# A fused two-layer decoder step on one core: routing scores moved into the gate steps, rows fetched four dots ahead, loads in parts

## What is computed

```python
q = (xb @ w_q).reshape(PEER_BLOCK, PEER_HEADS, 2, PEER_HALF)
s1 = jnp.einsum('thd,kd->thk', q[:, :, 0], sub_k1).astype(jnp.float32)
s2 = jnp.einsum('thd,kd->thk', q[:, :, 1], sub_k2).astype(jnp.float32)
v1, i1 = lax.top_k(s1, PEER_TOPK)
v2, i2 = lax.top_k(s2, PEER_TOPK)
cand = (v1[..., :, None] + v2[..., None, :]).reshape(PEER_BLOCK, PEER_HEADS, PEER_TOPK * PEER_TOPK)
top_s, top_pos = lax.top_k(cand, PEER_TOPK)
eidx = jnp.take_along_axis(cand_idx, top_pos, axis=-1)
gate = jax.nn.softmax(top_s, axis=-1)
u = expert_u[eidx]
act = jax.nn.gelu(jnp.einsum('thkd,td->thk', u, xb))
vv = expert_v[eidx]
return jnp.einsum('thk,thkd->td', (gate * act).astype(vv.dtype), vv)
```

## Time and profile before

| what | value |
|---|---|
| median of 3 runs | 3708.06 us (3708.01 to 3715.67) |
| span of the profiled execution | 3715.8 us |
| time around the span in that execution | not listed apart; the slowest of the runs, 3715.67 us, is as long as this span |
| TensorE busy | 3517.8 us (95%) |
| VectorE, ScalarE, GpSimd busy | 2481.2, 1361.9, 1842.5 us |
| mean granted clock of TensorE | 0.975 of full speed |
| phases s0 with routing, about | 436 to 1173 us |
| phase y0, about | 1175 to 1757 us |
| the same in layer 1, about | 2368 to 3095 and 3097 to 3700 us |

### The profile page before, as it was taken

One profiled execution on the slowest core, in us unless ns is written; L12 is line 12 of the kernel. 1 busy time (PEld: TensorE's weight loads), 2 busy tenths in 40 slices (PEclk: granted clock), 3 DMA queues, 4 the chain that ended last, 5 costly groups with the idle time before them and its releaser, 6 DMA issues.

```text
span 3715.8 us, 61775 instructions
## 1 busy us (share of the span) xinstructions
PE 3517.8 (95%) x21277; PEld 3348.0 (90%) x21277; DVE 2481.2 (67%) x5400; ACT 1361.9 (37%) x1938; POOL 1842.5 (50%) x1172
## 2 busy tenths in 40 slices
PE   7999999999999999999888689999999999999998
PEld 7999999999999999999773359999999999999998
DVE  3342597777775777775678543679697876777774
ACT  3322343534444333333221353344435353333332
POOL 3434456555655555552541234456565655555551
PEclk9999999999999999999998699999999999999999
DMA  3222367877788999994346322467777879999982
GB/s 131 80 69 91 103 188 247 277 247 262 262 281 274 298 310 313 324 320 154 99 116 179 105 74 91 136 193 249 268 240 277 274 282 277 297 326 311 329 295 97
DMA packets 392484, 812.36 MB, mean 219 GB/s; under 512 B 52104, under 2 KB 249672, under 8 KB 384888
## 3 DMA queue, kind: packets, MB, share of 16 engines
q1 hardware_dynamic: 171600, 458.35, 37.0%
q0 software_dynamic: 64608, 230.73, 18.1%
q10 hardware_dynamic: 156048, 120.37, 11.0%
HBM read 695.39 MB, written 112.74 MB: 217 GB/s over the span
## 4 chain that ended last, share of the span: by engine, by line
PE 66%; DVE 16%; DMA 7%; issue 4%; ACT 2%; POOL 2%; SPq 2%; another core or an unknown queue 0%; ACTq 0%; DVEq 0%; POOLq 0%
PE acc L638 42%; PE acc L625 15%; DMA rows<-u_in,expertP 4%; PE misc L774 3%; DVE rows L1838 3%; DMA raw<-slabs_in 2%; POOL w_lo L2274 1%; DVE misc L1773 1%; DVE route L1777 1%; DVE hot_gate L1876 1%; PE misc L814 1%; ACT w_hi L1104 1%; DVE work L1716 1%; DVE keyi L1724 1%; PE misc L843 1%
## 5 line engine op out<-in xcount | busy, mean ns | idle before, releaser
L2274 POOL TENSOR_TENSOR w_lo<-raw,w_hi 128x1024 fp32r<-128x1024 f32 x365 | 892.6, 2446 | 1079.8 <-ACT w_hi L1104 1078.6
L638 PE MATMUL acc<-h_hi,w_hi 128*128 128x416 f32 x3072 | 1097.7, 357 | 0.2 <-POOL h_lo L2316 0.2
L638 PE MATMUL acc<-h_lo,w_hi 128*128 128x416 f32 x3072 | 1085.9, 353 | 0.0
L638 PE MATMUL acc<-h_hi,w_lo 128*128 128x416 f32 x3072 | 1081.2, 352 | 0.0
L1104 ACT ACTIVATE w_hi<-raw 128x1024 fp32r<-128x1024 f32 x617 | 653.3, 1060 | 1090.0 <-DMA raw<-slabs_in 1045.4
L638 PEld LDWEIGHTS acc<-h_hi,w_hi 128*128 128x128 f32 x3072 | 581.2, 189 | 8.5 <-POOL h_lo L2316 0.6
L638 PEld LDWEIGHTS acc<-h_hi,w_lo 128*128 128x128 f32 x3072 | 581.9, 189 | 7.4
L638 PEld LDWEIGHTS acc<-h_lo,w_hi 128*128 128x128 f32 x3072 | 581.3, 189 | 3.9
L1955 DVE TENSOR_TENSOR w_lo<-raw,w_hi 128x1024 fp32r<-128x1024 f32 x252 | 325.4, 1291 | 206.1 <-ACT w_hi L1104 205.5
L1838 DVE CUSTOM_DVE_ANT_0 rows<-acc,rows 128x1024 f32<-128x1024 f32 (+1 forms) x224 | 273.4, 1221 | 205.9 <-DMA rows<-u_in,expertP 183.7
L638 PE MATMUL acc<-y_hi,w_hi 128*128 128x416 f32 x1024 | 362.1, 354 | 10.3 <-DVE y_lo L1947 4.3
(11 more groups left out here) (349 smaller groups left out, 5549.4 us busy)
## 6 DMA issues: line engine op xcount, KB each, us to landing
raw<-slabs_in SPq DMA_DIRECT2D x617, 512.0 KB
act_d<-gelu SPq DMA_DIRECT2D x256, 208.0 KB
gate_d<-gout SPq DMA_DIRECT2D x52, 1024.0 KB
abuf<-act_d ACTq DMA_DIRECT2D x32, 1664.0 KB
gbuf<-gate_d ACTq DMA_DIRECT2D x30, 1664.0 KB
unit<-ck_in SPq DMA_DIRECT2D x72, 128.0 KB
vquad<-cv_in SPq DMA_DIRECT2D x64, 128.0 KB
unit<-ck_in ACTq DMA_DIRECT2D x56, 128.0 KB
```

The source lines that it names most:

```text
L638: last = pe.matmul(acc[:, 0, par, 0:ND], w[:, c, :], m(c), start=c == 0 and w is w_hi[r] and m is m_hi, stop=c == KC - 1 and w is w_lo[r])
L2274: pool.tensor_tensor(w_lo[r][:], raw[r][:], w_hi[r][:].bitcast(F32), ALU.subtract).then_inc(lo_done, 1)
```

## The change

The edits are in the PEER part alone, and the same for both layers:

- Scores. Block 0's scores stay at the start. Those of block 1 go out in two pairs after slabs 18 and 20, those of blocks 2 and 3 in quarters of four products behind gate steps 4, 7, 10 and 13 of the block before, all through one bank (`quarter_scores`). ACT takes each quarter (`take_scores`), and may overwrite `sc` once `sums_done` says that VectorE has the candidates of the block before.
- Gate steps in three blocks of 16, at slabs 40, 72 and 104; the last 4 of the 52 at slabs 120 to 123 (`LAST_STEPS`). The four steps of block 0's tokens are the first of block 1's sixteen.
- Dots. 16 in the first window (twelve between the parts of `routing`, four behind it), 8 in each later one, 24 in each block of gate steps. In block 1's window the dots begin at the eighth place, and `expertP` is made at the fifth.
- Fetches. The fetch of row i goes out where dot i - 4 stands in the table, the first four at step 5; rows of groups 1 and up not before step 28.
- `hot_gate` is made from `iota` in SBUF and no longer from its copy in `misc`.
- Values: twelve in eleven slabs; groups begin and end at steps that a table gives.
- `act_d` and `gate_d` have other layouts: gates are stored in pieces of 512 bytes (8 KB before) and read in pieces of 3 KB and more (512 bytes before).
- A group's loads in y0 are eight parts spread over seven slabs. The last part of the first group's gates is loaded at step 124 (121 before), and group 1's parts at steps 124 to 126.
- The gelu of the dots and the product `weights` come after the first group's `weigh` and `low_part`.
- TensorE's gate steps are written out instead of looped.

```diff
+        HALVES = ND // HG
+        ROUTE_SLABS = [20, 20, 16, 16]
+        HALF_STEPS = 16
+        SLAB0 = [0, 20, 56, 88]
+        SCORE_STEPS = [4, 7, 10, 13]
-        WINDOW_DOTS = 12
-        STEP_DOTS = [[1] * 4, [1] * 4 + [0, 0] + [2, 1, 2, 1, 2, 2, 1, 2, 1, 2]]
+        WINDOW_DOTS = [16, 8, 8, 8]
+        STEP_DOTS = [1, 2, 1, 2, 1, 1, 2, 1, 2, 1, 2, 1, 2, 2, 1, 2]
+        at_slab = [6 + i for i in range(WINDOW_DOTS[0])]
...
-        FETCH_AT = [n - 2 for n in at_slab]
+        FETCH_AT = [5] * RB + at_slab[:-RB]
+        FETCH_AT = [n if i < TOPK else max(n, 28) for i, n in enumerate(FETCH_AT)]
...
+                    for r in range(HALF_STEPS):
+                        s_slab(0, done[0])
+                        done[0] += 1
+                        if r == TURN_STEP:
+                            group_h(2 * b)
+                        if r == HALF_STEPS - 1 and 2 * b + 1 < NGR:
+                            group_h(2 * b + 1)
+                        gates(H0 + HALF_STEPS * (b - 1) + r, r % 2)
+                        if r in SCORE_STEPS and b + 1 < NDB:
+                            if r == SCORE_STEPS[0]:
+                                pe.wait_ge(slotT_done, l * NDB + b + 1)
+                            quarter_scores(b + 1, SCORE_STEPS.index(r))
...
+                def load_part(j, par, part):
+
+                    if part % 2:
+                        b, i = divmod(part // 2, 2)
+                        act.dma_start(abuf[par][:, 4 * b + 2 * i:4 * b + 2 * i + 2],
+                                      act_d[l][2 * j + b][:, 2 * i:2 * i + 2]).then_inc(group_loaded[par], 16)
+                    else:
+                        n0, n1 = 6 * (part // 2), (6 * (part // 2) + 6 if part < 6 else NG)
+                        act.dma_start(gbuf[par][:, n0:n1], gate_d[l][j][:, n0:n1]).then_inc(group_loaded[par], 16)
...
-                    if n == NK - 7:
-                        load_first(STEP0[NDB - 1] // 2, NG)
-                        load_acts(1, 1)
-                    if n == NK - 5:
-                        load_gates(1, 1)
+                    if n == NK - 4:
+                        load_first(HALF_STEPS, NG)
+                    for part in {NK - 4: range(2), NK - 3: range(2, 5), NK - 2: range(5, 8)}.get(n, ()):
+                        load_part(1, 1, part)
...
-                    last = dve.tensor_scalar(hot_gate[par][:, t, :], count_row, idxT[:, 1, t0 + t:t0 + t + 1],
+                    last = dve.tensor_scalar(hot_gate[par][:, t, :], iota[:], idxT[:, 1, t0 + t:t0 + t + 1],
```

More of the change, by code:

```diff
@@ L466, in build @@
+        assert GROUP_END[-1] + 5 <= NK - 6
         N_CONST = 10
@@ L541, in peer_loads @@
                             if r % 2:
-                                half = q * 4 + (STEP0[b] - 4 * q1 + r + H0)
-                                store_gates(q * 2 + (STEP0[b] // 2 - 2 * q1 + r // 2), r // 2, half * 2 + 4)
-                    done[0] += STEPS_OF[b]
+                                half = q * 4 + (HALF_STEPS * (b - 1) - 4 * q1 + r + H0)
+                                store_gates(q * 2 + (HALF_STEPS * (b - 1) // 2 - 2 * q1 + r // 2), r // 2, half * 2 + 4)
+                    done[0] += HALF_STEPS
+                for n in range(done[0], done[0] + 4):
+                    step(n // 4, n % 4)
+                    if n in LAST_STEPS and n % 2:
+                        h = HALVES - 1 - (LAST_STEPS[-1] - n)
+                        store_gates(h // 2, h // 2 % 2, (H0 + h) * 2 + 4)
+                done[0] += 4
                 steps(NK - done[0])
@@ L827, in peer @@
                     last.then_inc(routeT_done, 1)
-                    if b:
-                        steps(b, 0, 4)
-                        group_h(2 * b)
-                        steps(b, 4, STEPS_OF[b] - 4)
-                    else:
-                        steps(b, 0, STEPS_OF[b])
+                scores(0, 0)
+                for j in range(2, 4):
+                    for k in range(4):
+                        ht = 4 * j + k
+                        last = pe.matmul(misc[:, j, k * P:(k + 1) * P], qT[:, ht, 0:P], subk[:, 2 * l + ht % 2, :],
+                                         start=True, stop=True)
+                    last.then_inc(score_done, 1)
+                pe.wait_ge(s_sc_taken, l + 1)
+                s_only(2)
+                group_h(0)
+                s_only(17)
+                scores(1, 0)
+                s_only(2)
+                scores(1, 1)
+                s_only(3)
+                turn_route(0)
+                s_only(4)
+                group_h(1)
+                s_only(SLAB0[1] + ROUTE_SLABS[1] - done[0])
+                for b in range(1, NDB):
+                    turn_route(b)
+                    if b == 1:
+                        pe.wait_ge(score_taken, 4 * (l * NDB + 2))
+                    for r in range(HALF_STEPS):
[10 more added lines that the diff above has]
+                            quarter_scores(b + 1, SCORE_STEPS.index(r))
+                    if b + 1 < NDB:
+                        s_only(ROUTE_SLABS[b + 1])
+                for r, n in enumerate(LAST_STEPS):
+                    s_slab(0, n)
+                    gates(H0 + 3 * HALF_STEPS + r, r % 2)
+                done[0] += len(LAST_STEPS)
                 s_only(NK - done[0])
@@ L1956, in weight_low @@
                         lo_done, 1)
+                for c in range(GRP):
+                    weigh(0, c)
+                for c in range(GRP):
+                    low_part(0, c)
                 dve.wait_ge(dot_act_done, 2 * (l + 1))
```

278 lines of the change are left out of this document (154 added, 124 removed).

## The result

The changed kernel takes 3739.2 us (median of 4 runs, 3738.1 to 3741.9) against 3710.4 us (3708.0 to 3715.7, 4 runs) before: a ratio of 1.0071, 95% interval 1.0053 to 1.0090. It is slower by about 29 us; the prediction had 3683, in the range 3645 to 3713. The profiled executions have spans of 3715.8 and 3736.3 us. They lie 20.5 us apart and not 29, since the one before was among its kernel's longer ones. These two are compared here.

A forecast was written before the change was run, and what follows sets the result against it. TensorE, busy 95%, loses idle and slow-clock time, mostly waiting for VectorE's route and gates in s0 and s1. 48.1 + 6 - 20.4 - 11.8 + 3 = 24.9 us gained: 3683 us median, range 3645 to 3713, own range 3668 to 3698.

The forecast's parts named there:

- Step 1, waits: Phases s0 and s1: with earlier scores and rows, all 24.7 us of route waits and 8.4 before the scores go.
- Step 1, clock: Phases s0 and s1: 15 us of half clock return with the removed waits; gain including those waits 48.1 us.
- Step 2, gate steps: Gate steps: rows four ahead and hot_gate from SBUF cut 18.3 us of waits; gain 6, bounds plus 18, minus 21.
- 12 us remain: Gate steps: what stays of TensorE's 18.3 us of waits, at block heads and where a new group of rows waits.
- rival C: Gate steps: hot_gate products and GpSimd's w_lo shut each other out, 3760 us; chance 0.16 together with a DMA limit.
- Step 3, block 0: Block 0: fetches waiting for dots delay GpSimd's w_lo; 17 us of waits, 3.4 half clock; cost 20.4, bounds 0 and 30.
- Step 4, end of s: End of s0 and s1: late last gates hold ACT's y_hi and slab 127's w_hi; cost 11.8 us, bounds 4 and 20.
- Step 5, y: y0 and y1: part of the waits for x and of the half clock returns; gain 3 us, bounds plus 5, minus 25.
- rival A: Whole kernel: no new waits, as dots keep ahead in block 0 or last gates land earlier; 3647 us; chance 0.24.

The follow-up runs named there:

- all five edits: Changed kernel with hot_gate's counter in PSUM, first 16 fetches early, index loads spread, value fetches two steps early, last gates four slabs earlier: 3653.4 us, ratio 0.9848.
- experiment 4: Changed kernel with SyncE's 24 routeP index loads spread over steps 24 to 27 instead of one piece ahead of step 24: 3723.2 us, ratio 1.0031.

## Why the prediction was wrong

Its sum for the profiled execution was a gain of 24.9 us; the loss was 20.5. By its steps:

Step 1, waits: right. 24.7 and 8.4 us went, and VectorE stands 11.0 us idle at the end of block 2's window, waiting only for the transposed route. That is the spare time foreseen, though 11 us and not 18.

Step 1, clock: too high. With the 6.8 booked against it in steps 3 and 4, a gain of 8 was forecast. By the granted clock the stretches at the 1.2 GHz level in phases s shrank from 37.6 to 30.7 us, and half of their length is what they cost: a gain of 3.4 us. TensorE's busy time there even rose, from 1415.0 to 1417.2. The stretches behind the route waits went, and the waits for w_lo made their own; those at slab 28 alone (6.8 us of length in each layer) cost 6.8 us and stood in no entry. Only with the waits away (all five edits) does the busy time fall to 1393.9, by 21 us, 18.8 of them the clock's; so the 15 us were there and were given back. The prediction's rule, a half clock after a wait of 2 us or more, is too sharp: in the kernel before, two waits of 2.17 us and one of 2.12 had none, and one of 1.87 had one. Its 1.7 us for a shorter stretch stands in no line of the earlier trace rows, whose two cost 3.3 and 3.4; the stretches of 3.4 us length in both traces bear it out.

Step 2, gate steps: this is the step that failed. "12 us remain" became 40.5; in place of a gain of 6 us the waits cost 22 more, just past the bound of minus 21 that the prediction drew and set aside. The mechanism is rival C's, which got too small a chance. Two terms were wrong. The saving by the operand in SBUF was taken from prob as 0.9 us a step; undisturbed it was 0.5 (2.63 to 2.12 us, one hot_gate 337 ns and not 285). And a hold-up was to cost nothing up to 1.6 us a step, on a sum of 4.7 us of VectorE's work in a step of 6.3. With 2.12 in place of 1.7 this sum is 5.1; with 3.2, the mean of the eight in the trace, it is 6.2, and nothing is spare. The products did not drift to where w_lo is not: in 53 of 104 steps they took over 3 us, mostly 4.2, which is 1.6 more than with PSUM. And at the head of a block and behind a change of group VectorE has no lead, so there each hold-up reached TensorE; these places are about 28 of the 40.5 us. Both signs that the prediction had set for step 2 came: waits for hot_gate over 25 us, and single hot_gate over 2 us.

The Trainium skill (SBUF — State Buffer, Who interferes with whom) says that a tensor_scalar in a two-port mode and a GpSimd instruction take a shared pair of ports in turn, each for a whole instruction, and that an operation with two inputs in SBUF contends as well with a GpSimd instruction that reads SBUF. The traces agree with both, by 4.21 against 2.12 us for the eight and by hot at up to 2.6 against 1.22 us. C's price, 77 us less the gain, was too high: half of the steps are hit. The share of steps was the number to ask for.

Step 3, block 0: mechanism right, size too high. The waits for w_lo there are 24.8 less 10.7 (slab 28) less 6.7 (slab 127), so 7.4 us, with three shorter ones of other names about 9.5, for 17 forecast. The first was longer than forecast (3.7 us at slab 10 for 2.5), and behind it came only 0.5 and 0.8 us where 1.8, 3.2 and 2.4 stood. The half clock was as booked, 3.4 us. The edit that takes all of it away gives about 10 us, where the step had 20.4. (A small slip in its working: from slab 13 at 507.4 us, six slabs of 4.5 us put slab 19 at 534.5 and not at 535.3.)

Missed altogether: slab 28. The prediction followed the queues of GpSimd, ACT and TensorE past the steps that move, and not SyncE's. Gate steps are also time in which prepared slabs last longer; moving four of them away uncovered 16 us of SyncE's work. The waits are 10.7 us, and experiment 4 gave about 15 with the clock. This term was put at nothing, and without a reason.

Step 4, end of s: mechanism right; 3.1 and 3.6 us for 4.0 each. In time, the edit that takes these waits away gave about 1 us alone and perhaps 10 with the others, for the 11.8 booked.

Step 5, y: plus 3 forecast, minus 5.5 measured, inside its bounds; the cause is open.

In sum for phases s: -33.1 + 22.2 + 7.4 + 10.7 + 6.7 + 0.7 (y_lo) comes to 14.6 us of waits, for 14.8 by which TensorE's idle time there grew; the other 2.3 us are its busy time. Without the operand the change is worth what the forecast's own range said (3668 to 3698): 0.9950 is 3692 us. That this falls in the range owes something to luck, since block 0 cost less than booked and slab 28 was not booked at all. And with its four faults mended (the operand, block 0's fetches, the index loads, the last gates) it comes near rival A's 3647: 0.9848 is 3654.

## What to carry to other kernels

Before an operand of a VectorE instruction is moved from PSUM to SBUF to save time, look for what GpSimd runs beside it: a saving of 0.5 us for eight instructions cost 45 us. When steps are moved, follow every engine's queue at the place that they leave, not only where they arrive; work that was hidden there keeps its length. When a hold-up is priced, the mean slack of a step is not enough: look for the places where the engine has no lead. And a gain of clock counts only when no new long wait comes, so it is booked last.
